# One kernel of a four-layer hybrid trunk: leftover keys turned four rows at once, the order inside the attention core, and one subtraction moved from GpSimd to VectorE

## The reference

```
s_idx = einsum('qhd,sd->qhs', qi, ki) * 64**-0.5
score = where(adm, einsum('qh,qhs->qs', wi, relu(s_idx)), -inf)
_, idx = top_k(score, n_sel)
logits = einsum('qgrd,qkgd->qgrk', q, k[idx]) * 64**-0.5 + bias
out    = einsum('qgrk,qkgd->qgrd', softmax(logits), v[idx]) @ w_o
```

## Time and profile before

| | us |
|---|---|
| median of 3 runs (lowest, highest) | 1799.42 (1798.11, 1799.64) |
| the profiled execution's own time | 1799.41 |
| its span, first to last instruction | 1797.6 |
| PE busy | 1773.3 (99%) |
| DVE busy | 1068.2 (59%) |
| ACT busy | 715.7 (40%) |
| POOL busy | 223.6 (12%) |
| mean granted clock of PE | 0.994 |

### The profile page before, as it was taken

The page is one execution under the profiler, slowest core; times in us unless marked ns, Lnnn a source line. Parts: engine busy times, 40 slices in busy tenths (PEclk is TensorE's granted clock), DMA queues, the critical chain, the costliest instruction groups (busy, mean ns, idle before and its releaser), DMA issues.

```text
span 1797.6 us, 27817 instructions
## 1 busy us (share of the span) xinstructions
PE 1773.3 (99%) x10014; PEld 1736.3 (97%) x10014; DVE 1068.2 (59%) x1848; ACT 715.7 (40%) x1139; POOL 223.6 (12%) x266
## 2 busy tenths in 40 slices
PE   9999999999999999999999999999999999999997
PEld 8988999999999999999999999999999889999997
DVE  7976855544587755554476655554458756555533
ACT  5366433333368433333222343333323554333331
POOL 5000300001235400001100200000140004000010
PEclk9999999999999999999999999999999999999998
DMA  8311333333333433334433333333454113433341
GB/s 304 121 36 60 111 123 122 123 119 128 122 111 106 132 129 118 124 114 136 139 117 117 119 118 125 121 124 120 136 187 161 48 48 95 133 132 118 129 141 59
DMA packets 63844, 216.96 MB, mean 121 GB/s; under 512 B 7153, under 2 KB 8769, under 8 KB 63521
## 3 DMA queue, kind: packets, MB, share of 16 engines
q1 hardware_dynamic: 59520, 202.25, 34.1%
q0 software_dynamic: 3280, 12.12, 2.2%
q10 hardware_dynamic: 976, 1.70, 0.3%
HBM read 212.38 MB, written 3.66 MB: 120 GB/s over the span
## 4 chain that ended last, share of the span: by engine, by line
PE 90%; DVE 6%; ACT 3%; issue 1%; DMA 0%; DVEq 0%; ACTq 0%
PE bank L705 26%; PE bank L704 26%; PE bank L703 26%; DVE w_lo L1308 2%; PE bank L903 1%; PE bank L859 1%; PE bank L880 1%; PE bank L861 1%; PE bank L860 1%; PE bank L922 1%; ACT w_hi L1026 1%; PE bank L886 1%; DVE work_b L1465 0%; DVE cv L1641 0%; PE bank L929 0%
## 5 line engine op out<-in xcount | busy, mean ns | idle before, releaser
L1308 DVE TENSOR_TENSOR w_lo<-raw,w_hi 128x1024 fp32r<-128x1024 f32 x382 | 490.4, 1288 | 312.3 <-ACT w_hi L1026 310.7
L703 PE MATMUL bank<-a_hi,w_hi 128*128 128x400 f32 (+2 forms) x1936 | 673.3, 348 | 1.1 <-DVE w_lo L1308 1.1
L704 PE MATMUL bank<-a_lo,w_hi 128*128 128x400 f32 (+2 forms) x1936 | 666.0, 344 | 0.0
L705 PE MATMUL bank<-a_hi,w_lo 128*128 128x400 f32 (+2 forms) x1936 | 665.3, 344 | 0.0
L1026 ACT ACTIVATE w_hi<-raw 128x1024 fp32r<-128x1024 f32 x382 | 399.9, 1052 | 345.7 <-PE bank L705 339.2
L703 PEld LDWEIGHTS bank<-a_hi,w_hi 128*128 128x128 f32 (+1 forms) x1936 | 362.5, 187 | 5.2 <-issue 1.2
L705 PEld LDWEIGHTS bank<-a_hi,w_lo 128*128 128x128 f32 (+1 forms) x1936 | 364.8, 188 | 0.6
L704 PEld LDWEIGHTS bank<-a_lo,w_hi 128*128 128x128 f32 (+1 forms) x1936 | 362.7, 187 | 2.6
L705 PE MATMUL bank<-h_hi,w_lo 128*128 128x400 f32 (+1 forms) x704 | 240.8, 342 | 0.0
L704 PE MATMUL bank<-h_lo,w_hi 128*128 128x400 f32 (+1 forms) x704 | 240.1, 341 | 0.0
L703 PE MATMUL bank<-h_hi,w_hi 128*128 128x400 f32 (+1 forms) x704 | 239.2, 340 | 0.0
(11 more groups left out here) (251 smaller groups left out, 1770.3 us busy)
## 6 DMA issues: line engine op xcount, KB each, us to landing
raw<-in_w_all SPq DMA_DIRECT2D x382, 512.0 KB, 3.5
bias_p<-rel_scratch POOLq DMA_DIRECT2D x2, 2176.0 KB, 11.0
k_s<-in_ck_t POOLq DMA_DIRECT2D x4, 512.0 KB, 8.6
v_c<-in_cv POOLq DMA_DIRECT2D x2, 1024.0 KB, 15.9
ki_s<-in_cki_t POOLq DMA_DIRECT2D x4, 256.0 KB, 5.4
x<-in_x_t SPq DMA_DIRECT2D x2, 400.0 KB, 6.4
x<-in_x_t ACTq DMA_DIRECT2D x2, 400.0 KB, 6.9
out_v_t<-v_f POOLq DMA_DIRECT2D x2, 400.0 KB, 5.0
```

The source lines that it names most:

```text
L703: pe.matmul(out, wh, hi[:, kc, c0:T], start=(first and n == 0), stop=False)
L704: pe.matmul(out, wh, lo[:, kc, c0:T], start=False, stop=False)
L705: mm = pe.matmul(out, wl, hi[:, kc, c0:T], start=False, stop=(last and n == len(blocks) - 1))
L1308: nc.vector.tensor_tensor(w_lo[:, s, :], raw[:, s, :], w_hi[:, s, :].bitcast(F32), ALU.subtract).then_inc(lo_ready, 1)
```

## The change

- **Leftover keys.** A prompt item now turns keys 16 and up (one piece for t = 0, two for t = 1), a sample item its 128 cached keys. The leftover 16 keys of the four items of a group are gathered by POOL in `few` (`few_keys`: 16 columns normalised at 32 s for slot s) and turned in one transpose more, after the group's last item. ACT copies the main pieces of a bank at once (four items of t = 0 or samples, two of t = 1), and the small bank in four pieces of 32 rows into `few_t`, zeroed elsewhere. `v_tok` gets matching tiles: the meta values four times and the new sample values of four streams, each at 32 partitions, spread by DVE into `v_p` before they are transposed. A sample group then multiplies `few_t` once over 512 columns rather than four times over 128. POOL zeroes `v_p` and `few_t`. Sample outputs are taken out in four views instead of two.
- **Order.** ACT's wait of gp = 1 for `unit_used` is gone. Before the core DVE now does two `take(1)` where it did three and the mask; the third comes in step 2, the mask in step 3, the `split` of unit 15 in step 0, and `take(2)` a step later each. `WO_TAIL` goes from 6 to 9: three more of the 64 `dense` blocks are left behind the last step.
- **Recurrent remainder.** `low(m)` runs on DVE instead of POOL, in the steps 3 to 11 of DVE's list.
- **Tail.** Twice five matmuls of 128 columns on constant ones, ahead of the waits for `last_sq`.

```diff
-WARM_UP = 24
+WARM_UP, TAIL_BUSY = 24, 5
...
+    for its in GROUPS[a]:
+        kind, _, what = its[0]
+        for s in range(len(its)):
+            if kind == "meta":
+                at.append((k, 0, True, None))
+                k += 1
+            elif kind == "prompt" and what[0]:
+                at.append((k, 256 * (s % 2), s % 2 == 1, k + 1 if s == 3 else None))
+                k += (0, 1, 0, 2)[s]
+            else:
+                at.append((k, 128 * s, s == 3, k + 1 if s == 3 else None))
+                k += (0, 0, 0, 2)[s]
...
+SLOT_COL = (0, 256, 128, 384)
...
-WO_TAIL = 6
+WO_TAIL = 9
...
-                return [(0, 0), (128, 1), (META + 128, 2)] if what[0] else [(0, 0), (META, 3)]
-            if kind == "sample":
-                return [(0, None), (128 - NQ * what, 4)]
-            return [(0, 0)]
+                return [META, META + 128] if what[0] else [META]
+            return [0]
...
+            def zeros_of_rows(a):
+                for v in lg:
+                    pool.memset(v[:], 0.0).then_inc(zeroed, 1)
+                pool.wait_ge(ss_done, 2 * LAYER_OF_A[a] + 1)
+                pool.memset(v_p[:], 0.0).then_inc(zeroed, 1)
+            def zeros_of_turned(a):
+                pool.wait_ge(wsum_done, NB * (a + 1))
+                pool.memset(few_t[0][:], 0.0)
+                pool.memset(few_t[1][:], 0.0).then_inc(zeroed, 1)
+            def few_keys(a):
+                for n, (kind, gp, _) in enumerate(ITEMS[a]):
+                    g, s = GROUP_OF[a][n], slot_of(a, n)
+                    if kind == "meta":
+                        continue
+                    pool.wait_ge(rinv_ready, IB[a] + n + 1)
+                    if fours(a, g) >= 2:
+                        pool.wait_ge(tr_done, uses_upto(a, fourth(a, fours(a, g) - 2)))
+                    c, b8 = (0 if kind == "prompt" else PAST), n % 8
+                    pool.tensor_scalar(few[fours(a, g) % 2][:, 32 * s:32 * s + 16], lg[n % NL][:, c:c + 16], rinv[:, b8:b8 + 1], None,
+                                       ALU.mult).then_inc(few_ready, 1)
...
-                def low(m):
-                    pool.wait_ge(conv_hi, m + 1)
-                    pool.tensor_tensor(b_lo[:, m, :], xc[:, m, :], b_hi[:, m, :].bitcast(F32), ALU.subtract).then_inc(xc_fed, 1)
...
-                                (low, 4), (tap, 6), (low, 5), (restart, 0), (tap, 7), (restart, 1), (low, 6), (low, 7),
-                                (restart, 2), (restart, 3)] + [(scale, m) for m in range(4)]:
+                for what, m in [(tap, m) for m in range(7)] + [(restart, 0), (tap, 7), (restart, 1), (restart, 2), (restart, 3)] + [
+                                (scale, m) for m in range(4)]:
...
+                    zeros_of_turned(a)
+                    few_keys(a)
...
+                    pe.wait_ge(v_spread, 2 * (a + 1))
+                    for n in range(5):
                         for ch in range(2):
                             col = 256 * (n % 2) + 128 * ch
-                            mm = pe.transpose(bank[5 + n // 2][:, col:col + 128], v_f[:, ch, c:c + 128], ident)
+                            if n < 2:
+                                src = v_f[:, ch, META + 128 * n:META + 128 * n + 128]
+                            else:
+                                src = v_p[:, ch, 4 * (n - 2):4 * (n - 2) + 4, :].rearrange("p b k -> p (b k)")
+                            mm = pe.transpose(bank[5 + n // 2][:, col:col + 128], src, ident)
...
-                    k, h, ends = USE[a][n]
-                    if h == 0:
+                    k, col, ends, small = USE[a][n]
+                    g, s = GROUP_OF[a][n], slot_of(a, n)
+                    if col == 0:
                         if k >= 2:
                             pe.wait_ge(pt_copied, UB[a] + k - 1)
                         else:
                             pe.wait_ge(scores_copied, a + 1)
                             pe.wait_ge(vt_ready, a + 1)
                     pe.wait_ge(pn_ready, IB[a] + n + 1)
-                    for i, (c, _) in enumerate(turned(ITEMS[a][n])):
-                        col = 256 * h + 128 * i
-                        mm = pe.transpose(bank[4 + k % 2][:, col:col + 128], lg[n % NL][:, c:c + 128], ident)
+                    for i, c in enumerate(turned(ITEMS[a][n])):
+                        mm = pe.transpose(bank[4 + k % 2][:, col + 128 * i:col + 128 * i + 128], lg[n % NL][:, c:c + 128], ident)
                     if ends:
                         mm.then_inc(tr_done, 1)
+                    if small is not None:
+                        if small >= 2:
+                            pe.wait_ge(pt_copied, UB[a] + small - 1)
+                        else:
+                            pe.wait_ge(vt_ready, a + 1)
+                        pe.wait_ge(few_ready, FB[a] + 4 * fours(a, g) + 4)
+                        pe.transpose(bank[4 + small % 2][:, 0:128], few[fours(a, g) % 2][:], ident).then_inc(tr_done, 1)
...
-                        tiles = turned(GROUPS[a][g][0])
+                        tiles = [0, 1, 2] if what[0] else [0, 2]
                         col = 128 * what[2]
-                        for i, (_, vt) in enumerate(tiles):
+                        for i in tiles:
                             for gi in range(2):
                                 v = 64 * (2 * gp + gi)
-                                mm = pe.matmul(ps[64 * gi:64 * gi + 64, col:col + 256], v_tok[:, vt, v:v + 64],
-                                               p[:, i, 256 * gi:256 * gi + 256], start=(i == 0), stop=(i == len(tiles) - 1))
+                                src = p[:, i, 256 * gi:256 * gi + 256] if i < 2 else few_t[g % 2][:, 256 * gi:256 * gi + 256]
+                                mm = pe.matmul(ps[64 * gi:64 * gi + 64, col:col + 256], v_tok[:, i, v:v + 64], src,
+                                               start=(i == 0), stop=(i == 2))
...
-                            cols = slice(128 * n, 128 * n + 128)
+                            cols = slice(SLOT_COL[n], SLOT_COL[n] + 128)
                             v = slice(128 * gp, 128 * gp + 128)
-                            pe.matmul(ps[:, cols], v_c[:, b, v], p[:, 0, cols], start=True, stop=False)
-                            mm = pe.matmul(ps[:, cols], v_tok[:, 4, v], p[:, 1, cols], start=False, stop=True)
+                            if n == 0:
+                                pe.matmul(ps[:], v_tok[:, 3 + b // 4, v], few_t[g % 2][:], start=True, stop=False)
+                            mm = pe.matmul(ps[:, cols], v_c[:, b, v], p[:, 0, cols], start=False, stop=(n == 3))
...
+            for _ in range(TAIL_BUSY):
+                pe.matmul(bank[7][:, 0:128], ones[:], ones[:], start=True, stop=True)
...
-                    if gp:
-                        act.wait_ge(unit_used, u0 + 17)
+                    act.wait_ge(zeroed, ZEROED * (a + 1))
...
+                            nc.scalar.activation(view[:, :, :, 0, :], ps[:].rearrange("p (r g q) -> p g r q", g=2, r=2),
                                                  ACT.Copy).then_inc(pt_copied, 1)
                     elif kind == "sample":
-                        c = 128 * (slot - 1)
-                        two = ps[:].rearrange("p (b i q) -> p i b q", b=2, i=2)
-                        nc.scalar.activation(p[:, 0, c:c + 256].rearrange("p (b q) -> p b q", b=2), two[:, 0], ACT.Copy)
-                        for s in range(2):
-                            b = what - 1 + s
-                            ins = nc.scalar.activation(p[:, 1, c + 128 * s:c + 128 * s + 128], two[:, 1, s], ACT.Copy,
-                                                       scale=cst[:, C_BSEL + b:C_BSEL + b + 1])
-                        ins.then_inc(pt_copied, 1)
+                        nc.scalar.activation(p[:, 0, :].rearrange("p (b1 b2 q) -> p b2 b1 q", b1=2, b2=2),
+                                             ps[:].rearrange("p (b2 b1 q) -> p b2 b1 q", b1=2, b2=2), ACT.Copy).then_inc(pt_copied, 1)
                     else:
                         nc.scalar.activation(p[0:META, 0, 0:128], ps[0:META, 0:128], ACT.Copy).then_inc(pt_copied, 1)
+                    if small is not None:
+                        act.wait_ge(tr_done, UB[a] + small + 1)
+                        for s in range(4):
+                            rows = slice(32 * s, 32 * s + 32)
+                            ins = nc.scalar.activation(few_t[g % 2][rows, SLOT_COL[s]:SLOT_COL[s] + 128], bank[4 + small % 2][rows, 0:128], ACT.Copy)
+                        ins.then_inc(pt_copied, 1)
...
-                    chain(nc.vector.tensor_copy(v_tok[96:128, 2:4, :].rearrange("p t c -> p (t c)"), bank[6][96:128, :]))
-                    nc.vector.memset(v_tok[96:112, 2:4, :], 0.0)
+                    nc.vector.tensor_copy(v_tok[:, 2:4, :].rearrange("p t c -> p (t c)"), bank[6][:])
                     nc.vector.tensor_copy(v_tok[:, 4, :], bank[7][:, 0:256]).then_inc(vt_ready, 1)
+                def spread():
```

(52 more changed lines are left out.)

58 lines of the change are left out of this document (25 added, 33 removed).

## The result

The changed kernel takes 1819.61 us (median of 4, 1816.08 to 1820.9), the one before 1799.53 us: a ratio of 1.0112 (95% interval 1.0095 to 1.0130), 20 us slower where 6 were forecast. One of the four executions of the kernel before took 2925.82 us, far off the others, and the ratio leaves it out. The profiled execution is the fastest of the four, 1816.08 us, span 1814.3, 16.7 above before. The sign was right, the time lies outside the range.

What follows compares the result with a forecast made beforehand. PE was taken to bound the kernel (busy 82.39 of 85 us in the first core). Gains of 17.3 us against new waits of 23.6 gave +6.3, from 1799.4 to 1805.7 us; the eight-in-ten range was 1790 to 1814.

Steps and rivals of the forecast that it cites:

- The ring: PE, DVE, ACT at group boundaries: late `tr_done` and copies make PE wait 0.43 + 0.82 us, 12 times, +15.0 us; splits extra.
- turns: PE's transposes in both cores: 72 fewer of 226, 0.107 us each, -7.7 us.
- values of samples: PE's sample groups: one matmul of 512 columns replaces four of 128; zero, between -2 and +0.5 us.
- begin: Begin of the cores: earlier start given back in full, 0 (to -3.9); low clock behind the second's begin goes, -1.7 us.
- halves: Where the halves meet: without ACT's wait, PE's waits and one stretch of low clock go, -5.3 us (-2.5 to -6).
- recurrent stage: `low` on DVE instead of POOL: PE's gap of 2.12 us shrinks, -1.8 us (0 to -3.8).
- The new gaps lower the clock: Rival: PE's boundary gaps bring low clock in four places, 1.7 us each, +6.8, 1812.5 us; chance 0.15.
- the splits of steps 9 and 25: DVE in each core: a `split` of 1.2 us inside the boundary's piece delays the next item in full, +4.8 us.
- slack in the ring: Rival: DVE or ACT run late by a step anyway, so the 12 boundaries cost nothing; 1790.7 us, chance 0.20.
- half price: Rival: only the first boundary wait, or both at half price, 7.8 us instead of 15; 1798.5 us, chance 0.15.
- a turn that frees its whole record: Rival: each removed transpose saves its full record on PE, 12 us more gain; 1793.7 us, chance 0.03.
- POOL and DVE: Rival: POOL's `few_keys` holds DVE up 0.44 us per item beside normalising, +10.5, 1816 us; chance 0.05.

Runs made afterwards that it cites:

- e1: The changed kernel, but `tr_done` rises at every turned item and DVE's `reduced(n)` waits for item n - 5 alone; 1792.67 us.
- e3: The changed kernel with ACT's copies as in the kernel before (two items or one) and DVE waiting for the use of item n - 5 alone; 1786.20 us.
- e4: As e3, but groups of t = 1 keep the changed kernel's wide copies; 1787.66 us.
- e9: e3's banks and copies, but DVE waits for the whole group in groups of t = 0 and samples, as in the changed kernel; 1804.76 us.
- e12: As e3, but in DVE's last step of a core `low` of the last group goes ahead of `half_out(7)`; 1783.48 us.
- e15: The kernel before with all of the change but the leftover keys, and with e12's place of `low`; 1785.00 us.

## Why the prediction was wrong

The mechanism that decides was forecast, with its place and its sign. The step that failed is "The ring", in its size: it priced a gap at its idle time alone and put at nothing what the end of PE's last matmul adds, 5.3 us over 32 gaps; its idle time was 2.2 short as well. Second, the low clock behind the new gaps (3.4 us in the profiled execution, some 7 in the median) was left out of the sum as a rival of 0.15. By steps, both cores, the profiled executions set against each other:

| step | forecast | measured |
|---|---|---|
| turns | -7.7 | -6.9 |
| values of samples, without clock | 0 | -0.2 |
| ring with the splits, idle time | +22.6 | +24.8 |
| ends of these 32 gaps | not seen | +5.3 |
| drain, with ends | +1.0 | +0.9 |
| begin, with ends, without clock | 0 | -1.3 |
| halves, without clock | -3.6 | -4.1 |
| clock at begin, halves and recurrent stage | -3.4 | -5.1 |
| clock at new gaps | 0 | +3.4 |
| end | 0 | +0.1 |
| recurrent stage, without clock | -1.8 | 0 |
| tail | -0.8 | -0.9 |
| sum | +6.3 | +16.0 (spans: +16.7) |

The 0.7 us that are missing from the sum are spread over the begins and small differences, and stay unexplained.

- **The ring.** 15.0 + 4.8 + 2.8 = 22.6 us of idle time were forecast, 24.8 were measured: the first gap 0.40 to 0.64 (forecast 0.43), the second 0.56 to 0.82 where nothing stands in the way (0.82), 1.8 to 2.0 with a `split`. What I left out is that PE's last matmul ahead of a gap no longer overlaps the next: 0.165 x 32 = 5.3 us. The rows of before had it: the last two records of a block lie 0.18 apart, ahead of a gap the step from one start to the end of the record is 0.34. The Trainium skill, "TensorE: Matmul & The Clock Gate", section "Single matmul latency", gives a single bf16 matmul a fixed share of 166 ns beyond its columns at the full clock. The 0.16 us here, for blocks and for transposes of float32, agree with it, as far as the profile's modelled ends go.
- **Clock.** "The new gaps lower the clock" had 0.15 and was written as a case of its own, when it is part of the first: four stretches were expected in it; the two profiled executions have two and four. The median lies another 3.5 us above the profiled execution; but even that one, the fastest with 1816.08, is above the 1814 of the range, so the clock of the other executions is not what took the time out of it.
- **Values of samples.** Right at full clock: 0.86 us for 512 columns (0.96 behind a wait), 1.67 to 1.77 per group, where it was 1.71 to 1.81. The 1.5 us more by starts are two groups in the low clock.
- **Recurrent stage.** The gap at 530 us went, as forecast, but two waits for `merged_low` (0.39 and 1.16 us) stand behind it now, where one of 0.45 was: DVE pays for `low` later. Without the clock the stage gains next to nothing; with it 1.7, against the 1.8 of the forecast. That its total came out is luck: the reason given for it (idle time of PE that goes, and a clock that gives nothing) was the wrong way round.
- **Right:** halves, end, tail, the splits of steps 9 and 25. (Those of steps 17 and 34 are four at 0.75 each, 3.0 and not the 2.8 of the sum.) Boundaries at which DVE waits are 14, not 12: the first ones count too.
- **Rivals that fell:** slack in the ring, half price, a turn that frees its whole record. POOL and DVE: `normalise` takes 287 ns over 128 keys where it took 296 over 144, so `few_keys` does not hold DVE up; it is POOL whose 0.42 us become 1.47 beside a `split` (10 of 96). The Trainium skill, "SBUF — State Buffer", "Who interferes with whom", has the two exclude each other; by this trace POOL is the one that waits (its record begins 0.13 to 0.2 us ahead of the `split`'s, whose 1.22 us stay what they are). PE never waits for POOL inside the cores, DVE for 0.8 us in all.

What stays open: which gaps lower the clock in a given execution, and why the begin's order is worth 0.7 us when its idle time says 1.4.

## What to carry to other kernels

When several small pieces are gathered into one bigger unit, look at each count that others wait for: a buffer that used to come free with its own piece now comes free with the last of the group. Keep the counting per item even if the work goes by groups; here that one semaphore was worth 27 us (20 of gaps, 7 of clock, the changed kernel against e1), the batching itself 2. And price every gap of TensorE at its idle time plus the end of the last matmul, and keep in mind that a long one may bring a stretch of low clock as well.

## What the runs showed of the hardware

- A gap of PE costs some 0.165 us beyond the idle time that the profile shows, whether a block (0.34 for 0.18) or a transpose (0.27 for 0.11) precedes it.
- Stretches of low clock (8 us at 0.79 in the mean) cost 1.7 us each, in a varying number for the same kernel. In the changed kernel they came behind gaps of 1.8 to 2.4 us. The profiled executions of e1 and e3, whose turns wait for 1.13 us at most, have none, and their executions lie within 0.4 us of each other. But short gaps are not safe: e4 has a stretch behind 0.38 and 1.17 us, 1.3 us apart, and single executions of e9, e12 and e15 lie 1.5 to 2 us above the fastest at a granted clock of 0.998 instead of 0.999.
- Four copies of 32 partitions x 128 columns on ACT take 0.26 us each, where one of 128 x 256 takes 0.37: 25.4 us in both cores for pieces of a quarter of the rows.
